# Residual additions of six tiles moved from VectorE to GpSimd at the end of a feed-forward

## The chip, the cores and the metric

One NeuronCore of one Trainium2 chip runs the whole program. The metric is the device time of one execution in microseconds (us); for a set of executions the median is given. Of the core's engines five matter here: TensorE (PE, matrix products and transposes), VectorE (DVE), ScalarE (ACT), GpSimd (POOL) and SyncE (SP), whose queue issues the transfers between memory and SBUF. Each engine works through its own program in order, and the engines are tied together by semaphores only. The profile names GpSimd POOL and VectorE DVE.

## What is computed

The program is one transformer block on a sequence of 1024 tokens with 1024 features, all in float32. It is a feed-forward, a mixer (sparse attention beside a recurrence), a cross attention to a memory, and a second feed-forward. Each is wrapped in norms and a residual. The change is in the end of the first feed-forward and in the norm that the mixer begins with:

```python
h = rms_norm(x, ffn1_pre_g[l])
x = x + 0.5 * rms_norm(swiglu(h, ffn1_w_gate[l], ffn1_w_up[l], ffn1_w_down[l]), ffn1_post_g[l])
h = rms_norm(x, mix_pre_g[l])
proj = h @ w_in[l]

def rms_norm(x, g):
    xf = x.astype(jnp.float32)
    y = xf * lax.rsqrt(jnp.mean(xf * xf, -1, keepdims=True) + NORM_EPS)
    return (y * g.astype(jnp.float32)).astype(x.dtype)
```

## The kernel before

`ffn_products` is called twice: for the first feed-forward (tag `f1`, with `next_gain`, so `after` is true) and for the second (tag `f2`, without it). The down projection lies token by feature: 8 tiles of 128 tokens by 1024 features, and each tile is two parts of 512 features (`m` = 2t and 2t + 1), which TensorE leaves in PSUM. Every float32 product is made of three passes over operands split into a high and a low half (`hi`, `lo`).

The end of the function is a software pipeline over tiles, written out by hand. In `step` s the engines do the following, each in this order:

- VectorE adds the last partial products of tile s onto `y` (L609, two instructions), then for tile s - 1 takes the reciprocal of the root (L619), multiplies by it and by the gain (L695, "scale") and adds the residual x in place (L699, "residual"); then for tile s - 2 the reciprocal of the next norm's root (L619) and its product with the gain (L705, "norm"); then for tile s - 3 the low halves of the transposed tile (L636, two instructions).
- ScalarE squares and sums tile s (L425) and takes the root (L427); then does the same over x of tile s - 1, for which it waits on the semaphore `x_added`; then copies the high halves of the transposed tile s - 3 to `hi` (L437, two instructions).
- TensorE transposes a tile when its norm is written (L781, eight matmuls) and then makes the products of the tile four further on (L715 to L717).
- SyncE stores each x tile when `x_added` has counted it, and loads x of tile t + 3 into the place of tile t - 1.

x lies in the four places of `f_raw`, scaled `y` in `one_y`, and the gains and normed tiles in `f_work`. Behind the stage there is a barrier of all engines (`core.clear`), and then `project_and_prepare` (names `fr_...`) begins. GpSimd has no work in this stage. Its float32 additions of another stage (L1248, 128 x 256, names `ar_...`) are the only two-input work that it does.

Of the kernel before, what the change touches and what calls it, by code (L numbers as in the profile page):

```python
# [16 lines left out]
ALU = mybir.AluOpType  # L17
# [85 lines left out]
def ffn_products(core, tag, w_gate, w_up, w_down, kept_dram, hi, lo, y, consts, x_in, x_out, post_gain, first_gain=None, next_gain=None, work=None,  # L103
# [8 lines left out]
    nc = core.nc  # L112
    ident, eps = consts["ident"], consts["eps"]
    F = w_gate.shape[1]
    PAIRS = F // (2 * P)
    LAST = PAIRS - 1
    before, after = first_gain is not None, next_gain is not None
    A11, A12, S2, S3, A22, S1, S4 = range(7)
    C11, C21, C22, C12 = range(4)
# [2 lines left out]
    with core.stage() as ctx:  # L122
# [60 lines left out]
        x_loaded = core.sems(f"{tag}_x_loaded", 4)  # L183
# [7 lines left out]
        scaled, x_added = core.sem(f"{tag}_scaled"), core.sem(f"{tag}_x_added")  # L191
        block = core.block(ctx)
# [7 lines left out]
        def split_at(i, s):  # L200
            return i * 7 + (s - 2)
# [13 lines left out]
        def of_tile(t):  # L215
            return slice(t * P, (t + 1) * P)
# [16 lines left out]
        def x_of(t):  # L233

            return raw[:].rearrange("p n (a k) f -> p (n a) (k f)", a=2)[:, t % 4, :]

        def turn_bank(n, t, h):
            bank = (4, 5, 6, 7) if n == 0 else (0, 1, 6, 7)
            return ps[:, bank[t % 2 * 2 + h], :].rearrange("p (k t) -> p k t", t=P)
# [5 lines left out]
        def _(sp):  # L245
# [13 lines left out]
            def keep(i, e):  # L259
                j, h = (0, 1, 1, 0)[e], (0, 0, 1, 1)[e]  # L260
                sp.wait_ge(prod_done, silu_at(i, e))
                sp.dma_start(kept_dram[bass.ds(i * 2 * P + j * P, P), h * HALF:(h + 1) * HALF], c[:, e, 1, :]).then_inc(kept[e], 16)

            def load_d(p):
                sp.dma_start(raw_d, d_dram[:, bass.ds(p * 2, 2), :]).then_inc(d_in, 16)

            def load_a(p):
                sp.dma_start(raw_a, a_dram[:, bass.ds(p * 2, 2), :]).then_inc(a_in, 16)
# [21 lines left out]
            for e in (C11, C21, C22):  # L290
                keep(1, e)
            with sp.Fori(2, LAST) as i:
                keep(i - 1, C12)
                sp.wait_ge(split_lo, split_at(i, A22))
                load_pair(i + 1)
                for e in (C11, C21, C22):
                    keep(i, e)
            keep(LAST - 1, C12)
            sp.wait_ge(split_lo, split_at(LAST, A22))
            load_d(0)  # L300
# [3 lines left out]
            for e in (C11, C21, C22, C12):  # L304
                keep(LAST, e)
            with sp.Fori(0, LAST - 1) as p:
                sp.wait_ge(down_lo, p * 4 + 2)
                load_d(p + 1)
                sp.wait_ge(down_lo, p * 4 + 4)
                load_a(p + 1)  # L310
            sp.wait_ge(down_lo, 4 * LAST - 2)
            load_d(LAST)
# [184 lines left out]
        def _(dve):  # L497
# [103 lines left out]
            def add(p, m, first=False):  # L601
                dve.wait_ge(dn_mm[m % 4], p * 4 + (m // 4 + 1))
                if first:
                    if m >= 8:
                        e = m // 2 - 4
                        dve.wait_ge(kept[e], kept_before(PAIRS, e))
                    nc.vector.tensor_copy(y[part(m)], down_bank(m)).then_inc(added[m % 4], 1)  # L607
                else:
                    nc.vector.tensor_tensor(y[part(m)], down_bank(m), y[part(m)], ALU.add).then_inc(added[m % 4], 1)  # L609
# [7 lines left out]
            def inverse(n, t):  # L617
                dve.wait_ge(rooted[n], t + 1)
                nc.vector.reciprocal(stats[:, n, 2, t:t + 1], stats[:, n, 1, t:t + 1]).then_inc(inverted[n], 1)  # L619
                dve.wait_ge(inverted[n], t + 1)  # L620
                return stats[:, n, 2, t:t + 1]
# [10 lines left out]
            def turned_lo(n, t):  # L632
                for h in range(2):
                    dve.wait_ge(hi_done[n], 2 * t + h + 1)
                    at = (slice(None), slice(4 * h, 4 * h + 4), of_tile(t))
                    nc.vector.tensor_tensor(lo[at], turn_bank(n, t, h), hi[at].bitcast(F32), ALU.subtract).then_inc(lo_done[n], 1)  # L636
# [48 lines left out]
            for step in range(TT + 3):  # L685
                t = step
                if t < TT:
                    add(LAST - 1, 2 * t)
                    add(LAST - 1, 2 * t + 1)
                t = step - 1  # L690
                if 0 <= t < TT:
                    rstd = inverse(1, t)
                    if t == 0:
                        dve.wait_ge(gains_in, 32 if after else 16)
                    nc.vector.scalar_tensor_tensor(out=y[:, t, :], in0=y[:, t, :], scalar=rstd, in1=g_post,  # L695
                                                   op0=ALU.mult, op1=ALU.mult).then_inc(scaled, 1)
                    dve.wait_ge(x_loaded[t % 4], 16 * (t // 4 + 1))
                    dve.wait_ge(scaled, t + 1)
                    nc.vector.tensor_tensor(x_of(t), x_of(t), y[:, t, :], ALU.add).then_inc(x_added, 1)  # L699
                t = step - 2  # L700
                if after and 0 <= t < TT:
                    rstd = inverse(2, t)
                    if t >= 2:
                        dve.wait_ge(turned[2], t - 1)
                    nc.vector.scalar_tensor_tensor(out=xn[:, t % 2, :], in0=x_of(t), scalar=rstd, in1=g_next,  # L705
                                                   op0=ALU.mult, op1=ALU.mult).then_inc(normed[2], 1)
                t = step - 3
                if after and t >= 0:
                    turned_lo(2, t)

        @block.tensor
        def _(pe):
# [2282 lines left out]
def block_kernel(nc, a, out):  # L2995
# [22 lines left out]
    with ExitStack() as ctx:  # L3018
        consts = make_consts(core, ctx, f["ident_"])

        def ffn(n, hi, lo, y, x_in, x_out, **gains):
            ffn_products(core, f"f{n}", f[f"ffn{n}_w_gate"], f[f"ffn{n}_w_up"], f[f"ffn{n}_w_down"], act, hi, lo, y, consts,
                         x_in, x_out, f[f"ffn{n}_post_g"], **gains)
# [92 lines left out]
```

## Time and profile before

| | |
|---|---|
| time, median of 3 executions | 2843.67 us (2841.96 to 2845.47) |
| the profiled execution: its own time | 2842.68 us |
| the profiled execution: span of the trace | 2840.8 us |
| mean granted TensorE clock | 0.976 |
| PE busy | 2683.6 us (94%) |
| DVE busy | 1756.1 us (62%) |
| ACT busy | 968.1 us (34%) |
| POOL busy | 88.0 us (3%) |

The shares are means over stages with different limits. TensorE is the busy engine of the whole, and a single stage can be held by another one. The stage with the change lies between 672 and 735 us of the span. In the timeline a row gives the start, the duration, the engine, the line and the operation, and in brackets the idle time before it with what ended it. Starts of successive instructions on an engine are closer than their durations, since they overlap a little.

### The profile page before, as it was taken

What the parts mean: (1) busy time and instruction counts of PE and PEld (TensorE: products, weight loads), DVE (VectorE), ACT (ScalarE), POOL (GpSimd) and SP (SyncE); (2) the same over time, 40 slices, a digit from 0 to 9 for tenths busy, and PEclk for the clock granted to TensorE, in tenths of its full rate; (3) what the DMA queues carried; (4) which work ended last, traced back from release to release, by engine and by line L of the source; (5) the groups of instructions that cost most, each with busy time, mean ns of one, the idle gap of its engine ahead of it and who ended that gap; (6) DMA issues with size and microseconds to landing.
All of it is one profiled execution on the core that took longest, in us unless ns stands there. A gap on an engine that the chain in (4) does not pass through costs nothing. (4 is left out here: it accounts for less than half of the span.)

```text
span 2840.8 us, 47378 instructions
## 1 busy us (share of the span) xinstructions
PE 2683.6 (94%) x19368; PEld 2214.9 (78%) x19368; DVE 1756.1 (62%) x2869; ACT 968.1 (34%) x1731; POOL 88.0 (3%) x121
## 2 busy tenths in 40 slices
PE   6999999999799999699999998899997999999998
PEld 5888887887577778588888886687775888887887
DVE  5866665767444472277777775753444856666666
ACT  4332222113333433244444444442432323222122
POOL 0000000000000000111111110000000000000000
PEclk9999999999899999799999999999998999999999
DMA  4222223224423385611111110530031222223224
GB/s 138 82 85 74 74 85 107 104 103 153 102 86 97 107 271 140 164 43 40 40 35 29 36 40 26 212 127 1 30 119 56 82 89 85 74 73 119 103 89 156
DMA packets 230632, 260.91 MB, mean 92 GB/s; under 512 B 63426, under 2 KB 186560, under 8 KB 230464
## 3 DMA queue, kind: packets, MB, share of 16 engines
q1 hardware_dynamic: 228880, 256.91, 28.3%
q8 instruction: 124, 2.03, 0.3%
q10 hardware_dynamic: 1584, 1.60, 0.2%
q14 instruction: 44, 0.36, 0.0%
HBM read 189.17 MB, written 64.06 MB: 89 GB/s over the span
## 5 line engine op out<-in xcount | busy, mean ns | idle before, releaser
L715 PE MATMUL f_ps<-hi,f_wh 128*128 128x512 f32 x768 | 302.1, 393 | 19.3 <-DVE f_wl L501 11.9
L717 PE MATMUL f_ps<-hi,f_wl 128*128 128x512 f32 x768 | 300.8, 392 | 0.0
L715 PE MATMUL f_ps<-f_t1h,f_wh 128*128 128x512 f32 x480 | 187.1, 390 | 0.0
L716 PE MATMUL f_ps<-f_t1l,f_wh 128*128 128x512 f32 x480 | 186.8, 389 | 0.0
L715 PEld LDWEIGHTS f_ps<-hi,f_wh 128*128 128x128 f32 x768 | 145.5, 189 | 52.4 <-issue 10.7
L2051 PE MATMUL fr_dense_ps<-hi,fr_wh 128*128 128x512 f32 x400 | 167.0, 417 | 7.1 <-DVE fr_wl L2342 7.1
L717 PEld LDWEIGHTS f_ps<-hi,f_wl 128*128 128x128 f32 x768 | 145.5, 189 | 30.4
L715 PE MATMUL f_ps<-f_t2h,f_t3h 128*128 128x512 f32 x384 | 151.6, 395 | 7.8 <-DVE one_y L607 3.7
L2052 PE MATMUL fr_dense_ps<-one_lo,fr_wh 128*128 128x512 f32 x400 | 156.8, 392 | 0.0
L2053 PE MATMUL fr_dense_ps<-hi,fr_wl 128*128 128x512 f32 x400 | 156.8, 392 | 0.0
L716 PE MATMUL f_ps<-f_t2l,f_t3h 128*128 128x512 f32 x384 | 150.9, 393 | 0.0
L717 PE MATMUL f_ps<-f_t2h,f_t3l 128*128 128x512 f32 x384 | 150.7, 393 | 0.0
L716 PE MATMUL f_ps<-two_lo,f_wh 128*128 128x512 f32 x384 | 150.5, 392 | 0.0
L716 PE MATMUL f_ps<-one_lo,f_wh 128*128 128x512 f32 x384 | 150.4, 392 | 0.0
L609 DVE TENSOR_TENSOR y<-f_ps,y 128x512 f32<-128x512 f32 x144 | 99.2, 690 | 61.7 <-PE f_ps L717 61.7
L549 DVE TENSOR_TENSOR one_y<-f_ps,one_y 128x1024 f32<-128x1024 f32 x60 | 72.5, 1222 | 100.4 <-PE f_ps L717 100.4
L549 DVE TENSOR_TENSOR y<-f_ps,y 128x1024 f32<-128x1024 f32 x60 | 72.5, 1222 | 100.3 <-PE f_ps L717 100.3
L609 DVE TENSOR_TENSOR one_y<-f_ps,one_y 128x512 f32<-128x512 f32 x144 | 98.7, 689 | 56.0 <-PE f_ps L717 56.0
L717 PE MATMUL f_ps<-f_t1h,f_wh 128*128 128x512 f32 x320 | 124.5, 389 | 0.0
L2740 PE MATMUL mt_d_ps<-mt_wh,hi 128*128 128x512 f32 x224 | 94.6, 423 | 20.4 <-DVE two_lo L2933 19.0
L2342 DVE TENSOR_TENSOR fr_wl<-one_y,fr_wh 128x1024 fp32r<-128x1024 f32 x41 | 50.1, 1221 | 96.3 <-ACT fr_wh L2207 96.2
L715 PEld LDWEIGHTS f_ps<-f_t1h,f_wh 128*128 128x128 f32 x480 | 90.1, 188 | 18.5
(419 smaller groups left out, 6458.8 us busy)
## 6 DMA issues: line engine op xcount, KB each, us to landing
one_y<-in_w_in SPq DMA_DIRECT2D x25, 512.0 KB, 4.4
f_raw<-in_ffn_w_gate SPq DMA_DIRECT2D x11, 1024.0 KB, 5.4
f_raw<-in_ffn_w_up SPq DMA_DIRECT2D x11, 1024.0 KB, 7.9
act<-one_y SPq DMA_DIRECT2D x44, 256.0 KB, 2.1
f_raw<-in_ffn_w_down SPq DMA_DIRECT2D x11, 1024.0 KB, 4.9
f_raw<-act SPq DMA_DIRECT2D x11, 1024.0 KB, 4.8
early<-in_ffn_w_gate SPq DMA_DIRECT2D x11, 1024.0 KB, 5.4
early<-in_ffn_w_up SPq DMA_DIRECT2D x11, 1024.0 KB, 7.9
```

Of the source, the lines that this page charges most:

```text
L549: nc.vector.tensor_tensor(out, a, b, op).then_inc(joined, 1)
L609: nc.vector.tensor_tensor(y[part(m)], down_bank(m), y[part(m)], ALU.add).then_inc(added[m % 4], 1)
L715: nc.tensor.matmul(out, wh, xh, start=start, stop=False)
L716: nc.tensor.matmul(out, wh, xl, start=False, stop=False)
L717: return nc.tensor.matmul(out, wl, xh, start=False, stop=stop)
L2051: nc.tensor.matmul(dense_ps[:, b, cols], w_hi[:, b, k, :], hi[:, k, cols], start=(k == 0), stop=False)
L2052: nc.tensor.matmul(dense_ps[:, b, cols], w_hi[:, b, k, :], lo[:, k, cols], start=False, stop=False)
L2053: mm = nc.tensor.matmul(dense_ps[:, b, cols], w_lo[:, b, k, :], hi[:, k, cols], start=False, stop=(k == KD - 1))
L2342: nc.vector.tensor_tensor(w_lo[:, c % 2], raw[:, c % 2], w_hi[:, c % 2].bitcast(F32), ALU.subtract).then_inc(lo_split, 1)
L2740: mm = nc.tensor.matmul(bank(n, b), lhsT[:, k, at], rhs[:, k, to], start=(k == 0 and x_ == 0), stop=(k == KD - 1 and x_ == 2))
```

## The change

For the first feed-forward `BY_POOL` is 6, for the second 0. GpSimd gets a program of its own for the stage: for each of the tiles 0 to 5 it waits until x is loaded and `y` is scaled, and adds. VectorE keeps the additions of tiles 6 and 7, and ahead of tile 6 it waits until all six of GpSimd have been counted on `x_added`, which both engines increment.

```diff
+    BY_POOL = 6 if next_gain is not None else 0
...
                     nc.vector.scalar_tensor_tensor(out=y[:, t, :], in0=y[:, t, :], scalar=rstd, in1=g_post,
                                                    op0=ALU.mult, op1=ALU.mult).then_inc(scaled, 1)
-                    dve.wait_ge(x_loaded[t % 4], 16 * (t // 4 + 1))
-                    dve.wait_ge(scaled, t + 1)
-                    nc.vector.tensor_tensor(x_of(t), x_of(t), y[:, t, :], ALU.add).then_inc(x_added, 1)
+                    if t >= BY_POOL:
+                        dve.wait_ge(x_loaded[t % 4], 16 * (t // 4 + 1))
+                        dve.wait_ge(scaled, t + 1)
+                        if t == BY_POOL and BY_POOL:
+                            dve.wait_ge(x_added, BY_POOL)
+                        nc.vector.tensor_tensor(x_of(t), x_of(t), y[:, t, :], ALU.add).then_inc(x_added, 1)
...
+        @block.gpsimd
+        def _(pool):
+            for t in range(BY_POOL):
+                pool.wait_ge(x_loaded[t % 4], 16 * (t // 4 + 1))
+                pool.wait_ge(scaled, t + 1)
+                nc.gpsimd.tensor_tensor(x_of(t), x_of(t), y[:, t, :], ALU.add).then_inc(x_added, 1)
```

VectorE's program in step 4 of the stage, before (lines of the kernel before):

```order
L609 TENSOR_TENSOR one_y<-f_ps,one_y 128x512 [waits f1_dn_mm0]
L609 TENSOR_TENSOR one_y<-f_ps,one_y 128x512 [waits f1_dn_mm1]
L619 RECIPROCAL f_stats<-f_stats 128x1 [waits f1_rooted1]
L695 SCALAR_TENSOR_TENSOR one_y<-one_y,f_stats,f_work 128x1024 [waits f1_inverted1]
L699 TENSOR_TENSOR f_raw<-f_raw,one_y 128x1024 [waits f1_scaled,f1_x_loaded3]
L619 RECIPROCAL f_stats<-f_stats 128x1 [waits f1_rooted2]
L705 SCALAR_TENSOR_TENSOR f_work<-f_raw,f_stats,f_work 128x1024 [waits f1_turned2,f1_inverted2]
L636 TENSOR_TENSOR one_lo<-f_ps,hi 128x4x128 [waits f1_hi_done2] x2
```

The same step on VectorE now (lines of the changed kernel, one to four further on):

```order
L610 TENSOR_TENSOR one_y<-f_ps,one_y 128x512 [waits f1_dn_mm0]
L610 TENSOR_TENSOR one_y<-f_ps,one_y 128x512 [waits f1_dn_mm1]
L620 RECIPROCAL f_stats<-f_stats 128x1 [waits f1_rooted1]
L696 SCALAR_TENSOR_TENSOR one_y<-one_y,f_stats,f_work 128x1024 [waits f1_inverted1]
L620 RECIPROCAL f_stats<-f_stats 128x1 [waits f1_rooted2]
L709 SCALAR_TENSOR_TENSOR f_work<-f_raw,f_stats,f_work 128x1024 [waits f1_turned2,f1_inverted2]
L637 TENSOR_TENSOR one_lo<-f_ps,hi 128x4x128 [waits f1_hi_done2] x2
```

The residual has gone from between scale and norm, so the reciprocal and the norm of the tile before follow scale directly.

GpSimd's program from the stage's beginning to the next stage's now, of which only the last two rows were there before:

```order
L720 ISA
L720 TENSOR_TENSOR f_raw<-f_raw,one_y 128x1024 [waits f1_scaled,f1_x_loaded0]
L720 TENSOR_TENSOR f_raw<-f_raw,one_y 128x1024 [waits f1_scaled,f1_x_loaded1]
L720 TENSOR_TENSOR f_raw<-f_raw,one_y 128x1024 [waits f1_scaled,f1_x_loaded2]
L720 TENSOR_TENSOR f_raw<-f_raw,one_y 128x1024 [waits f1_scaled,f1_x_loaded3]
L720 TENSOR_TENSOR f_raw<-f_raw,one_y 128x1024 [waits f1_scaled,f1_x_loaded0]
L720 TENSOR_TENSOR f_raw<-f_raw,one_y 128x1024 [waits f1_scaled,f1_x_loaded1]
L123 UNCONDITIONAL_BRANCH
L2046 UNCONDITIONAL_BRANCH [waits barrier_Pool_Activation_PE_DVE_SP_gather]
L2048 MEMSET fr_w_full 64x512
```

The six additions now stand alone on GpSimd, each behind the scale of its own tile. ScalarE's program in a step has the same rows as before (here step 4's, lines of the changed kernel):

```order
L426 ACTIVATE f_junk,f_stats<-one_y 128x1024 [waits f1_summed1,f1_added1,f1_added0]
L428 ACTIVATE f_stats<-f_stats,eps 128x1 [waits f1_summed1]
L426 ACTIVATE f_junk,f_stats<-f_raw 128x1024 [waits f1_summed2,f1_x_added]
L428 ACTIVATE f_stats<-f_stats,eps 128x1 [waits f1_summed2]
L438 CAST hi<-f_ps 128x4x128 [waits f1_turned2]
L438 CAST hi<-f_ps 128x4x128
```

Nothing moved on it: the square over x, which waits on `x_added`, still stands ahead of the copies to `hi`.

## Rows read from the trace of the kernel before

**Rows 1.** Timeline, VectorE, step 4 of the stage (start us, us)

```profile
694.98 1.28 DVE L609 TENSOR_TENSOR one_y<-f_ps,one_y 128x512 f32<-128x512 f32 x2
696.17 0.15 DVE L619 RECIPROCAL f_stats<-f_stats 128x1 f32<-128x1 f32 x1
696.36 1.28 DVE L695 SCALAR_TENSOR_TENSOR one_y<-one_y,f_stats,f_work 128x1024 f32<-128x1024 f32 x1
697.75 1.23 DVE L699 TENSOR_TENSOR f_raw<-f_raw,one_y 128x1024 f32<-128x1024 f32 x1
698.89 0.16 DVE L619 RECIPROCAL f_stats<-f_stats 128x1 f32<-128x1 f32 x1
699.09 1.28 DVE L705 SCALAR_TENSOR_TENSOR f_work<-f_raw,f_stats,f_work 128x1024 f32<-128x1024 f32 x1
701.00 1.29 DVE L636 TENSOR_TENSOR one_lo<-f_ps,hi 128x512 fp32r<-128x512 f32 x2 [0.63 <-ACT hi L437]
702.20 1.28 DVE L609 TENSOR_TENSOR one_y<-f_ps,one_y 128x512 f32<-128x512 f32 x2
```

**Rows 2.** Timeline, ScalarE, the same step

```profile
699.01 1.06 ACT L425 ACTIVATE f_junk<-f_raw 128x1024 bf16<-128x1024 f32 x1 [1.19 <-DVE f_raw L699]
...
700.19 0.29 ACT L427 ACTIVATE f_stats<-f_stats,eps 128x1 f32<-128x1 f32 x1
700.40 1.05 ACT L437 CAST hi<-f_ps 128x512 fp32r<-128x512 f32 x2
```

**Rows 3.** Busy time by windows: PE, PEld, DVE, ACT, POOL, clock, DMA

```profile
694.98:702.20 7.22, 7.22 (x39) 6.09 (x38) 6.42 (x10) 3.85 (x8) 0.00 (x0) 1.00 0.52 178
...
716.64:723.85 7.21, 1.77 (x8) 1.57 (x8) 6.41 (x10) 3.85 (x8) 0.00 (x0) 0.76 0.18 73
```

**Rows 4.** Timeline, VectorE, scales of tiles 0 and 1, norm of tile 0

```profile
679.90 1.28 DVE L695 SCALAR_TENSOR_TENSOR one_y<-one_y,f_stats,f_work 128x1024 f32<-128x1024 f32 x1 [3.99 <-DMA f_work<-in_mix_pre_g]
...
683.82 1.29 DVE L695 SCALAR_TENSOR_TENSOR one_y<-one_y,f_stats,f_work 128x1024 f32<-128x1024 f32 x1
...
686.55 1.28 DVE L705 SCALAR_TENSOR_TENSOR f_work<-f_raw,f_stats,f_work 128x1024 f32<-128x1024 f32 x1
```

**Rows 5.** Timeline, TensorE, transposes of tiles 0 and 1

```profile
687.89 1.09 PE L781 MATMUL f_ps<-ident,f_work 128*128 128x128 f32 x8 [2.15 <-DVE f_work L705]
...
694.30 1.03 PE L781 MATMUL f_ps<-ident,f_work 128*128 128x128 f32 x8
```

**Rows 6.** One line: GpSimd's additions elsewhere, duration ns min/median/max

```profile
L1248 POOL TENSOR_TENSOR ar_LTm<-ar_GB,ar_m_lev x80: 715/732/1129, 1194.6 to 1700.0; 128x256 f32<-128x256 f32 x80
```

**Rows 7.** Groups of GpSimd instructions by shape: busy us, mean ns

```profile
L1242 POOL MEMSET ar_win<- 128x512 f32 x1 | 0.5, 526 | 0.0
...
L1241 POOL MEMSET ar_M<- 128x256 f32 x1 | 0.3, 312 | 441.7 <-POOLq L69 441.7
...
L1243 POOL MEMSET ar_kc<- 128x2 f32 x1 | 0.1, 97 | 0.0
```

**Rows 8.** Timeline, VectorE and GpSimd, near 1314 us

```profile
1314.06 0.42 DVE L1574 TENSOR_TENSOR ar_L<-ar_ps,ar_m_low 128x256 f32<-128x256 f32 x1 [0.38 <-PE ar_ps L1347]
...
1315.61 0.84 DVE L1621 TENSOR_TENSOR ar_TT<-ar_TT,ar_eye 128x256 f32<-128x256 f32 x1
...
1314.56 0.73 POOL L1248 TENSOR_TENSOR ar_T<-ar_L,ar_m_one 128x256 f32<-128x256 f32 x1 [53.79 <-DVE ar_L L1574]
1315.25 0.92 POOL L1248 TENSOR_TENSOR ar_LTm<-ar_GB,ar_m_lev 128x256 f32<-128x256 f32 x1
```

**Rows 9.** Timeline, VectorE and GpSimd, near 1463 us

```profile
1463.30 0.41 DVE L1619 TENSOR_TENSOR ar_TT<-ar_GB,ar_m_one 128x256 f32<-128x256 f32 x1
...
1463.46 0.84 POOL L1248 TENSOR_TENSOR ar_T<-ar_L,ar_m_one 128x256 f32<-128x256 f32 x1 [0.49 <-DVE ar_L L1574]
```

**Rows 10.** Timeline, VectorE's last of the stage, ScalarE's first of the next

```profile
734.64 0.68 DVE L636 TENSOR_TENSOR one_lo<-f_ps,hi 128x512 fp32r<-128x512 f32 x1
...
738.15 1.99 ACT L2207 CAST fr_wh<-one_y 128x1024 fp32r<-128x1024 f32 x2 [3.66 <-PEq L69]
```

**Rows 11.** Busy time by windows, the next stage's first 14 us

```profile
738.00:752.00 14.00, 11.50 (x43) 9.37 (x44) 3.29 (x5) 1.99 (x2) 0.52 (x1) 0.78 0.68 129
```

## The prediction

> **What bounds the stage now.** I read the windows of the stage first, then the timeline of one step on VectorE, then the same step on ScalarE, and last every place in the trace where GpSimd adds. TensorE leads the whole kernel, but in this stage the beat is VectorE's: one step takes 7.22 us, VectorE is busy 6.42 us of it, and the step repeats unchanged when TensorE has run dry (1.77 us busy) [rows 3]. TensorE's own work on a tile takes 694.30 - 687.89 = 6.41 us [rows 5].
>
> VectorE still idles 0.63 us in the step, and it waits there for ScalarE [rows 1]. So the closed loop is not VectorE's work alone. From the step's start to the end of scale is 697.64 - 694.98 = 2.66 us. The residual starts 0.11 later and takes 1.23 [rows 1]. ScalarE's square over x starts 0.03 behind it (699.01 against 698.98), the copy to hi comes 1.39 after that (700.40), VectorE's low half 0.60 later (701.00), and the next step 1.20 later (702.20) [rows 1, 2]. The sum is 2.66 + 0.11 + 1.23 + 0.03 + 1.39 + 0.60 + 1.20 = 7.22. The residual is a link of that loop, because on ScalarE the copies for tile s - 3 stand behind the square over x of tile s - 1, and VectorE's low half waits for the copies. The norm (1.28 us) lies beside this loop, not on it.
>
> **What the change does to the loop.** It takes 1.23 us of work from VectorE but leaves the residual where it was in the chain: scale, then residual, then ScalarE. The link 0.11 + 1.23 becomes a hand-over to GpSimd plus GpSimd's duration P. The hand-over: a DVE addition ends at 1314.48 and GpSimd starts at 1314.56, 0.08 us [rows 8]. A step of the loop is then 5.96 + P, and it changes by P - 1.26.
>
> P is not in the trace at 128 x 1024. GpSimd's 128 x 256 addition has a median of 732 ns [rows 6], and 0.73 us where nothing disturbs it [rows 8]. From above, four of these are 2.92 us. From below, its MEMSET grows by 526 - 312 = 214 ns for 256 elements [rows 7]; an addition that grew no faster would take 0.73 + 3 x 0.214 = 1.37. MEMSET reads nothing, so I hold to the upper end and take off only the fixed part, which MEMSET of 2 elements shows as 0.097 [rows 7]: P = 2.92 - 3 x 0.10 = 2.62 us. A larger fixed part makes P smaller.
>
> The Trainium skill (GPSIMD Engine Reference, "Performance versus the Vector engine") gives 4497 ns for an addition of 2048 float32, and calls GpSimd about half as fast as VectorE at it. Half of that is an estimate of 2.25 us for this tile, and by it the sum below would be +4.3 us. The trace agrees with the direction, 0.73 against VectorE's 0.42 at 256 elements [rows 8].
>
> **Does the freed VectorE run undisturbed?** Near 1315 us VectorE's addition of two SBUF operands took 0.84 [rows 8], while the same shape took 0.41 elsewhere [rows 9]. It ended (1316.45) 0.28 behind GpSimd's (1316.17), and GpSimd's took 0.92 instead of 0.73. So of two such additions one waits almost until the other is done, and a held VectorE instruction ends 0.13 less than its own length behind GpSimd's end. Scale and norm also have two SBUF operands; the additions of L609 and the low halves of L636 have one, the other lies in PSUM. The Trainium skill (SBUF, "Who interferes with whom") says it as a rule: a VectorE instruction with two SBUF inputs and a GpSimd instruction that reads SBUF exclude each other, and whoever starts first holds the port to its end. The trace agrees, by the 0.84 and 0.92. A rule without this exclusion would take the first term below from +1.05 to below nothing.
>
> **Steps 1 and 2, where time could be won.** Scale of tile 0 ends at 681.18 [rows 4], GpSimd's addition runs 681.26 to 683.88. VectorE, freed of its residual, does the two additions of step 2 and asks for scale of tile 1 near 682.5, 1.3 us before its old start, but is held: it ends at 683.88 + 1.28 - 0.13 = 685.03, against 685.11 before [rows 4]. GpSimd takes tile 1 from 685.11 to 687.73. Norm of tile 0 needs ScalarE's root, which comes at 683.88 + 0.03 + 1.39 = 685.30, so it asks after GpSimd has begun and is held again: it ends at 687.73 + 1.15 = 688.88, against 687.83 [rows 4]. That is +1.05 us, and TensorE, which idles 2.15 us for this norm [rows 5], idles 3.2.
>
> **Steps 3 to 6.** Each has GpSimd's addition in the loop: 4 x (2.62 - 1.26) = 5.44 us. ScalarE's other square of the step (1.39) ends before GpSimd does and is hidden by it. TensorE's 6.41 per tile stays under the new step of 8.58. The norm, held by GpSimd, ends near 3.8 us behind scale; the low half starts 4.7 behind it, so it is covered.
>
> **Steps 7 to 10** are as before: residuals 6 and 7 are VectorE's, and the added wait for six counts on x_added was met a step earlier. The stores follow x_added in order. The load of x for tile 4 waits for norm 0 and starts some 1.1 us later, and its tile is wanted more than 10 us after that. GpSimd's empty slot has nothing else in it. The six instructions left out of VectorE need no other cover. The barrier and the next stage start 2.8 us after VectorE's last low half [rows 10] and move with it.
>
> **Sum.** 1.05 + 5.44 = +6.5 us. P stands in it six times (twice in the first term, four times in the second), so in general it is 6.5 + 6 x (P - 2.62): -1.0 at P = 1.37, +8.3 at 2.92. The profiled execution took 2842.68 us, 1.9 more than its span. 2842.68 + 6.5 = 2849.2. The median of the executions shown lies 0.99 above it, so the forecast for a median is 2850.2. What this kernel's timing can tell from no change I take as 0.2%, 5.7 us; the sum passes it where P is over 2.49.
>
> **The rivals.**
>
> 1. *VectorE's norm gets the port first in steps 3 to 6.* Behind scale GpSimd starts at +0.08. The norm follows at +0.11, as behind the residual now (699.09 against 698.98 [rows 1]), with the reciprocal overlapped. 0.03 us decide. Near 1463 us VectorE was 0.16 ahead and ran its full 0.41, GpSimd took 0.84 instead of 0.73: the port was free 0.27 after VectorE's start, 0.14 short of its length [rows 9]. By this a norm ahead holds GpSimd for 0.03 + 1.14 = 1.17 us a step, four times 4.7: +11.2, 2854.9 us. For it speaks how narrow the lead is, against it that GpSimd has the lead. In step 2 it cannot happen, the norm is late there by ScalarE.
> 2. *The other side: GpSimd's addition is mostly a fixed cost.* Were P the 0.73 of 256 elements, the loop would lose 0.53 a step, and the sum would be 6.5 + 6 x (0.73 - 2.62) = -4.8, 2838.9 us. The sign turns at P = 1.54. MEMSET's growth from 97 to 526 ns speaks against it [rows 7]. Beating the kernel before by 0.2% would need P under 0.6.
> 3. *TensorE loses its clock, or GpSimd starts slowly.* TensorE would idle 2.2 us in each step of 8.6. At 1.77 us busy of 7.21 the granted clock fell to 0.76 on the mean, at full work it was 1.00 [rows 3]. At 1.2 GHz a tile's 6.41 would be 12.8, more than the step by 4.2, in four steps some 17 us. Alternatively the first addition pays once. GpSimd's first addition of this stage stands behind an instruction that readies it (ISA in its program) by some 670 us. The Trainium skill (GPSIMD Engine Reference, "Instruction dispatch") has about 6 us for the first call into freshly loaded code; no row here shows it.
>
> **How the numbers follow.** The forecast's case (GpSimd first, P from 2.0 to 2.9) has a chance of 0.54 and gives 2846.5 to 2852; the part of it over 0.2% has 0.30, the part under has 0.24, since P sits near the edge. Rival 1 has 0.28, all of it slower. Rival 2 with all P under 2.0 has 0.10: 0.02 faster, 0.08 within 0.2%. Rival 3 has 0.08, slower. Slower is 0.30 + 0.28 + 0.08 = 0.66, same 0.32, faster 0.02. The range goes from P = 2.0 (+2.8, 2846.5) to rival 1 with P = 2.8 (+12.3, 2856); it leaves out rival 2 and rival 3. Where the next stage's first matmuls meet the clock's return (0.78 on the mean of its first 14 us [rows 11]) can move either figure by about a microsecond.
>
> **What would show it.** In the changed trace: six GpSimd additions of 2.3 to 2.9 us; steps 3 to 6 of 8.3 to 8.9 us from one pair of L610 to the next, with ScalarE's square over x waiting for GpSimd; VectorE's wait before L637 grown from 0.63 to above 2 us or taken up by a norm of some 3.6 us; scale of tile 1 shown as some 2.5 us long; step 7 at 7.2 us again. Wrong I would be if the additions are under 1.6 us, if GpSimd's rows are near 3.8 us and the norms 1.28 (rival 1), if a matmul in steps 3 to 6 takes double, or if the next stage takes back what this one loses.

## The result and the profile after

The changed kernel takes 2847.78 us, the kernel before 2841.97 us (medians of 20 executions each, taken in turn). The ratio is 1.0020 with a 95% interval of 1.0014 to 1.0026, so the change costs 5.8 us. Forecast were 6.5 us more and 2850.2 in the range 2846.5 to 2856.0; the before it was added to, 2843.67, lies 1.7 above the median of the larger set.

The profiled executions have spans of 2846.1 and 2840.8 us. A whole kernel of this length varies by some microseconds from one execution to the next, so from here on the stage is measured inside one trace: from the start of the first scale (L695 before, L696 now) to the start of the last low halves (L636, L637). That is 734.03 - 679.90 = 54.13 us before and 738.04 - 678.59 = 59.45 now, 5.32 us more. In these two traces the rest of the span evens out: the first scale comes 1.31 earlier, and what lies behind the stage takes 1.3 longer.

The page of the changed kernel shows where work went. VectorE should have lost 6 x 1.23 = 7.4 us and has 4.5 more than before (1756.1), GpSimd has 14.1 more (88.0):

```profile
PE 2684.6 (94%) x19368; PEld 2215.1 (78%) x19368; DVE 1760.6 (62%) x2863; ACT 967.5 (34%) x1731; POOL 102.1 (4%) x127
```

VectorE in step 4 of the changed kernel, in the timeline, beside [rows 1]:

```profile
695.41 1.28 DVE L610 TENSOR_TENSOR one_y<-f_ps,one_y 128x512 f32<-128x512 f32 x2
696.61 0.15 DVE L620 RECIPROCAL f_stats<-f_stats 128x1 f32<-128x1 f32 x1
696.80 1.29 DVE L696 SCALAR_TENSOR_TENSOR one_y<-one_y,f_stats,f_work 128x1024 f32<-128x1024 f32 x1
698.00 0.16 DVE L620 RECIPROCAL f_stats<-f_stats 128x1 f32<-128x1 f32 x1
698.19 3.51 DVE L709 SCALAR_TENSOR_TENSOR f_work<-f_raw,f_stats,f_work 128x1024 f32<-128x1024 f32 x1
702.64 1.29 DVE L637 TENSOR_TENSOR one_lo<-f_ps,hi 128x512 fp32r<-128x512 f32 x2 [0.94 <-ACT hi L438]
703.84 1.28 DVE L610 TENSOR_TENSOR one_y<-f_ps,one_y 128x512 f32<-128x512 f32 x2
```

The step is 703.84 - 695.41 = 8.43 us long instead of 7.22. The residual is gone, and the norm that follows directly has grown from 1.28 to 3.51: what VectorE was to be spared, it now spends on a norm that has started and is held until GpSimd's addition is done. GpSimd's rows of tiles 1 to 3:

```profile
683.66 2.34 POOL L720 TENSOR_TENSOR f_raw<-f_raw,one_y 128x1024 f32<-128x1024 f32 x1 [1.23 <-DVE one_y L696]
689.82 2.38 POOL L720 TENSOR_TENSOR f_raw<-f_raw,one_y 128x1024 f32<-128x1024 f32 x1 [3.81 <-DVE one_y L696]
698.23 2.39 POOL L720 TENSOR_TENSOR f_raw<-f_raw,one_y 128x1024 f32<-128x1024 f32 x1 [6.04 <-DVE one_y L696]
```

Scale ends at 698.09, GpSimd starts 0.14 later and ends at 700.62; the norm ends at 701.70, 1.08 behind it. ScalarE in the same step, beside [rows 2]:

```profile
700.65 1.06 ACT L426 ACTIVATE f_junk<-f_raw 128x1024 bf16<-128x1024 f32 x1 [2.40 <-POOL f_raw L720]
...
702.04 1.05 ACT L438 CAST hi<-f_ps 128x512 fp32r<-128x512 f32 x2
```

It waits for GpSimd now, 0.03 behind its end, and its copies are what VectorE's low halves wait for. The chain is the one of before with a slower link. The windows of steps 4 and 5 and of step 7, beside [rows 3]:

```profile
695.41:703.84 8.43, 8.31 (x45) 6.81 (x43) 7.42 (x9) 3.85 (x8) 2.39 (x1) 1.00 0.41 142
703.84:712.25 8.41, 6.58 (x33) 5.25 (x32) 7.40 (x10) 3.85 (x8) 2.37 (x1) 1.00 0.35 123
720.66:727.86 7.20, 1.77 (x8) 1.57 (x8) 6.42 (x10) 3.85 (x8) 0.00 (x0) 0.60 0.19 74
```

Step 7, where the residual is VectorE's again, is 7.20 long (7.21 before). VectorE's busy time per step has risen from 6.42 to 7.42 with less to do; 2.2 us of what is shown as busy is the norm being held. The first steps, beside [rows 4]:

```profile
681.18 2.33 DVE L696 SCALAR_TENSOR_TENSOR one_y<-one_y,f_stats,f_work 128x1024 f32<-128x1024 f32 x1
...
684.17 2.91 DVE L709 SCALAR_TENSOR_TENSOR f_work<-f_raw,f_stats,f_work 128x1024 f32<-128x1024 f32 x1
```

Scale of tile 1 and norm of tile 0 are both held, 2.33 and 2.91 instead of 1.28. Behind them TensorE's transpose starts (its row, beside [rows 5], and the window after it):

```profile
687.14 1.20 PE L792 MATMUL f_ps<-ident,f_work 128*128 128x128 f32 x8 [3.19 <-DVE f_work L709]
```

```profile
687.10:690.40 3.30, 3.26 (x14) 2.78 (x15) 3.23 (x6) 1.82 (x5) 0.58 (x1) 0.64 1.03 292
```

TensorE idled 3.19 us instead of 2.15, as forecast, and then something came that was not in the sum: the granted clock in the 3.3 us behind is 0.64, that is 1.2 GHz for most of it, where before it was 1.00 all through. This is inside step 3, and the starts of the 128 x 512 matmuls stand 0.43 us apart there, 0.23 later in the same step.

### The profile page after: what moved, and what is told of

It is laid out like the page before. It is cut to its first block and busy times, and to the rows that moved or that the text cites. A ratio compares the mean times of both kernels' runs of the same rounds, so it can differ in the third digit from the quotient of the medians.

```text
span 2846.1 us, 47378 instructions
## 1 busy us (share of the span) xinstructions
PE 2684.6 (94%) x19368; PEld 2215.1 (78%) x19368; DVE 1760.6 (62%) x2863; ACT 967.5 (34%) x1731; POOL 102.1 (4%) x127
## 5 line engine op out<-in xcount | busy, mean ns | idle before, releaser
L610 DVE TENSOR_TENSOR y<-f_ps,y 128x512 f32<-128x512 f32 x144 | 99.1, 689 | 61.6 <-PE f_ps L728 61.6
L610 DVE TENSOR_TENSOR one_y<-f_ps,one_y 128x512 f32<-128x512 f32 x144 | 98.7, 689 | 56.0 <-PE f_ps L728 56.0
L727 PEld LDWEIGHTS f_ps<-f_t1l,f_wh 128*128 128x128 f32 x480 | 90.4, 188 | 18.7
```

Of the source, the lines that this page charges most:

```text
L727: nc.tensor.matmul(out, wh, xl, start=False, stop=False)
```

## The experiments

Each run e1 to e10 was executed 11 times (e2 5 times) in turn with the kernel before, in three sets (e1 to e4, e5 to e8, e9 and e10); the changed kernel's row is that of the section before. "Stage" is the length defined above, from one trace of each kernel.

| run | stage us | against 54.13 | ratio to before, 95% interval |
|---|---|---|---|
| changed kernel | 59.45 | +5.32 | 1.0020 (1.0014 to 1.0026) |
| e1_two_tiles | 55.23 | +1.10 | 1.0002 (0.9993 to 1.0011) |
| e2_late_start | 64.13 | +10.00 | 1.0035 (1.0022 to 1.0049) |
| e3_half_add | 52.99 | -1.14 | 0.9995 (0.9986 to 1.0004) |
| e4_thin_add | 47.76 | -6.37 | 0.9979 (0.9970 to 0.9988) |
| e5_copies_first_before | 49.83 | -4.30 | 0.9984 (0.9975 to 0.9993) |
| e6_copies_first_after | 54.02 | -0.11 | 0.9995 (0.9986 to 1.0004) |
| e7_lows_first_after | 55.13 | +1.00 | 1.0005 (0.9996 to 1.0014) |
| e8_late_six | 52.67 | -1.46 | 0.9997 (0.9988 to 1.0006) |
| e9_lows_first_to_seven | 49.56 | -4.57 | 0.9986 (0.9977 to 0.9995) |
| e10_middle_five | 48.65 | -5.48 | 0.9980 (0.9971 to 0.9989) |

One per mille is 2.84 us. In every row the stage's difference lies inside the interval of the whole kernel, so within some 2.6 us (3.8 for e2) what the stage loses or wins goes through to the end. The five runs whose interval holds 1 are told apart by the stage alone.

### Is the residual a link of the loop, and what is it worth per microsecond?

e1 leaves GpSimd only the tiles ahead of the loop:

```diff
-    BY_POOL = 6 if next_gain is not None else 0
+    BY_POOL = 2 if next_gain is not None else 0
```

> BY_POOL is 2 instead of 6, so GpSimd adds for tiles 0 and 1 alone. The stage from the first scale to the start of the last low halves took 54.13 us before and 59.45 with six tiles. Theory A (the residual is a link of the loop from step 3 on, each step there pays 1.2 us, steps 1 and 2 together 0.57): 54.7, and 0.0% to 0.05% over the kernel before. Theory B (each tile on GpSimd costs the same, 5.32 / 6 = 0.89): 55.9.

Measured was 55.23, between the two. Up to the additions of step 3 the stage is the changed kernel's (8.43 and 8.42 behind the first scale; before 7.85), so steps 1 and 2 cost 0.57 as in theory A, and steps 5 to 7 are 7.22 long again. The other 0.5 came in step 4:

```profile
694.45 0.68 DVE L610 TENSOR_TENSOR one_y<-f_ps,one_y 128x512 f32<-128x512 f32 x1
695.57 0.69 DVE L610 TENSOR_TENSOR one_y<-f_ps,one_y 128x512 f32<-128x512 f32 x1 [0.44 <-PE f_ps L728]
```

VectorE waits for a product here, since TensorE's matmuls behind its idle time of 2.76 us ran at the lower clock (granted 0.65 in the 3.3 us from 687.4). The two rows of its timeline are a matmul behind the transpose and one 3.3 us later:

```profile
688.66 0.63 PE L727 MATMUL f_ps<-f_t1l,f_wh 128*128 128x512 f32 x1
...
691.94 0.39 PE L726 MATMUL f_ps<-f_t2h,f_t3h 128*128 128x512 f32 x1
```

So theory B, the same cost for every tile, falls: two tiles ahead of the loop cost 0.57, each of the four in the loop 1.20, and a longer TensorE wait can add half a microsecond through the clock. In the changed kernel no L610 of the stage waits for a product; that last part is covered by the longer steps.

e3 and e4 leave the hand-overs as they are and shorten GpSimd's addition; they leave out the rest of the residual. This is e3's edit, and e4 has `0:2` in place of `0:HALF`:

```diff
-                nc.gpsimd.tensor_tensor(x_of(t), x_of(t), y[:, t, :], ALU.add).then_inc(x_added, 1)
+                nc.gpsimd.tensor_tensor(x_of(t)[:, 0:HALF], x_of(t)[:, 0:HALF], y[:, t, 0:HALF], ALU.add).then_inc(x_added, 1)
```

> The changed kernel with GpSimd adding only features 0 to 511 of each of its six tiles (the other half of the residual is left out). Theory A (GpSimd's duration stands in the stage six times, and breaks even near 1.2 us): the addition takes 1.28 us, a step of 3 to 6 takes 7.3, steps 1 and 2 gain 1.6, the stage 52.9, 1.2 under the kernel before. Theory B (a fixed cost of the hand-over between engines is what is lost): steps near 8.4 still, the stage over 58.

> The changed kernel with GpSimd adding only 2 features of each of its six tiles (the rest of the residual is left out), so that the loop keeps its hand-overs but almost no duration. Theory A: the loop would take 6.2 us, less than TensorE's 6.41 for a tile, so TensorE becomes the bound: steps 3 to 6 at 6.4, the stage 48.5 to 49.5, 0.15% to 0.2% under the kernel before. Theory B (hand-overs are what is lost): the stage no shorter than 54.

The half addition took 1.29 us, the step 7.33, the stage 52.99 (52.9 expected). The thin one, of 2 features, took 0.20, the step 6.23 to 6.33, the stage 47.76, less than the 48.5 to 49.5 expected: steps 1 and 2 gained 2.64 (5.21 us from the first scale to the additions of step 3), and steps 3 and 4 took the loop's own 6.23, not yet TensorE's 6.33 to 6.42 from one transpose to the next. Theory B of both, that the hand-over itself is what is lost, falls. In step 5 of the thin run VectorE and GpSimd read:

```profile
701.29 1.30 DVE L709 SCALAR_TENSOR_TENSOR f_work<-f_raw,f_stats,f_work 128x1024 f32<-128x1024 f32 x1
...
701.32 0.20 POOL L720 TENSOR_TENSOR f_raw<-f_raw,one_y 128x2 f32<-128x2 f32 x1 [6.08 <-DVE one_y L696]
```

With 0.20, 1.29 and 2.38 us for 2, 512 and 1024 elements, GpSimd's addition is 0.19 us plus 2.13 ns an element. From 1024 to 512 elements the stage fell by 6.46 us for 1.09 us of duration, 5.9 times as much: the factor 6 of the prediction.

### Who gets the port?

In the changed kernel the norm starts 0.04 us ahead of GpSimd (698.19 against 698.23), and still it is the norm that waits. The port is the access to SBUF that, as the prediction has it, the two engines share. e2 lets GpSimd ask a little later (`late` is a small tile of its own):

```diff
                 pool.wait_ge(scaled, t + 1)
+                nc.gpsimd.memset(late[:, 64 * t:64 * t + 64], 0.0)
                 nc.gpsimd.tensor_tensor(x_of(t), x_of(t), y[:, t, :], ALU.add).then_inc(x_added, 1)
```

> The changed kernel with one GpSimd MEMSET of 128 x 64 between the wait for scale and each addition, so that GpSimd asks for its operands some 0.15 us later than now, when VectorE's norm starts 0.04 us ahead of it and yet waits for it. Theory A (the port goes to whoever asks first, and VectorE lost by a few hundredths): the norms of steps 3 to 6 fall back to 1.28 us, GpSimd's additions there rise from 2.38 to about 3.4, a step takes 9.6 instead of 8.41, the stage 64.5. Theory B (GpSimd always wins, whoever starts first): norms stay near 3.5 us, only the MEMSET's own 0.15 is added per step, the stage 60.4. The first addition comes right behind the instruction that readies GpSimd for it: if that costs once, tile 0's is longer by some microseconds, otherwise 2.4.

The timeline of VectorE and GpSimd in step 4 of that run:

```profile
699.32 1.28 DVE L710 SCALAR_TENSOR_TENSOR f_work<-f_raw,f_stats,f_work 128x1024 f32<-128x1024 f32 x1
704.87 1.29 DVE L638 TENSOR_TENSOR one_lo<-f_ps,hi 128x512 fp32r<-128x512 f32 x2 [4.27 <-ACT hi L439]
```

```profile
699.33 0.15 POOL L721 MEMSET f_late<- 128x64 f32 x1 [6.01 <-DVE one_y L697]
699.43 3.42 POOL L722 TENSOR_TENSOR f_raw<-f_raw,one_y 128x1024 f32<-128x1024 f32 x1
```

The norm is back at 1.28, GpSimd's addition takes 3.42, and VectorE's wait before the low halves is 4.27. The step is 9.5 us, the stage 64.13 (64.5 expected). This is rival 1 of the prediction, brought about by a tenth of a microsecond: with 0.11 of a lead VectorE wins, with 0.04 GpSimd does. Theory B falls. The instruction that readies GpSimd stands at 679.8 to 679.9 us in this run and the first addition right behind it, at 679.94; it took 2.40, as long as the undisturbed additions of the changed kernel (2.34 to 2.41), so no such start cost shows here. In the changed kernel that instruction stands at 3.1 us, and the first addition took 2.41.

### Is it the order on ScalarE that puts the residual in the loop?

e5 swaps two pieces of ScalarE's program in the kernel before, and e6 in the changed kernel; both compute the whole:

```diff
+                t = step - 3
+                if after and t >= 0:
+                    turned_hi(2, t)
                 t = step - 1
                 if after and 0 <= t < TT:
                     act.wait_ge(x_added, t + 1)
                     rms(2, t, x_of(t), 1.0 / D, 0)
-                t = step - 3
-                if after and t >= 0:
-                    turned_hi(2, t)
```

> The kernel before with one change on ScalarE: in each step the copies to hi of tile s - 3 stand ahead of the square over x of tile s - 1. Theory A (the residual is in the loop only because of that order): the wait of 0.63 us ahead of the low halves goes, a step is VectorE's own work, 1.20 + 0.19 + 1.39 + 1.15 + 0.19 + 1.20 + 1.20 = 6.52 instead of 7.22, the stage 50.0 instead of 54.13, 0.15% under the kernel before. Theory B (ScalarE's copies come late for another reason): steps stay at 7.2, the stage at 54.

The end of step 4 on VectorE in e5:

```profile
699.18 1.28 DVE L705 SCALAR_TENSOR_TENSOR f_work<-f_raw,f_stats,f_work 128x1024 f32<-128x1024 f32 x1
700.39 1.28 DVE L636 TENSOR_TENSOR one_lo<-f_ps,hi 128x512 fp32r<-128x512 f32 x2
701.59 1.28 DVE L609 TENSOR_TENSOR one_y<-f_ps,one_y 128x512 f32<-128x512 f32 x2
```

The wait of 0.63 is gone, the step is 6.51 and the stage 49.83 (50.0 expected): three lines in another place bring 4.3 us, on the kernel before and without GpSimd.

> The changed kernel with the same swap on ScalarE. GpSimd's addition is then no link of the loop of the low halves. Theory A (the norm, held by GpSimd until it is done, takes its place on VectorE): 2.66 + 0.14 + 2.37 + 1.08 - 0.08 + 1.20 = 7.4 a step in steps 3 to 6, 6.5 in steps 7 and 8, the stage 54 to 54.5. Theory B (exclusion by GpSimd costs nothing once the order is right): TensorE's 6.41 a step, the stage 50.

```profile
698.86 3.51 DVE L709 SCALAR_TENSOR_TENSOR f_work<-f_raw,f_stats,f_work 128x1024 f32<-128x1024 f32 x1
702.29 1.27 DVE L637 TENSOR_TENSOR one_lo<-f_ps,hi 128x512 fp32r<-128x512 f32 x2
```

With six tiles on GpSimd the same swap leads to a step of 7.41 and a stage of 54.02. The low halves no longer wait for ScalarE; they stand directly behind a norm of 3.51 us. That is 4.2 us more than e5. 3.6 of it lie in steps 3 to 6 (7.41 against 6.51), and there the low halves wait for no copy: the exclusion, that one engine is held while the other adds, keeps the freed VectorE from being faster. The other 0.6 are those of steps 1 and 2.

### Can the freed time be used at all?

e7 gives VectorE work with one operand in SBUF to do beside GpSimd's addition, in place of the norm: on top of e6, `turned_lo(2, step - 3)` stands ahead of the norm of `step - 2`.

> As the run before, and on VectorE the low halves of tile s - 3 (one operand in SBUF, one in PSUM) stand ahead of the norm of tile s - 2, beside GpSimd's addition. Theory A: what was waiting for GpSimd in vain is filled with work that doesn't exclude it, 2.66 + 0.14 + 2.37 + 1.08 - 0.08 = 6.2 a step on VectorE, so that TensorE's 6.41 is the bound in steps 3 to 6; with the 0.6 of steps 1 and 2 the stage takes 50 to 50.5. Theory B (low halves are held by GpSimd too): steps of 7.4 or more, the stage over 54.

e8 has the order of e7, with `for t in range(2, TT)` on GpSimd and tiles 0 and 1 on VectorE.

> As the run before, but with tiles 2 to 7 on GpSimd and tiles 0 and 1 on VectorE, so that the norm for which TensorE idles isn't held and TensorE doesn't idle longer than in the kernel before. Theory A: the 0.57 of steps 1 and 2 and the matmuls at half clock behind the longer idle time go, steps 3 on at TensorE's 6.4, the stage 49 to 49.8, the shortest that computes the whole. Theory B (GpSimd on the last two tiles lies on the closing chain, where nothing is left to put beside it, 1.2 us a tile): the stage 51 to 52.

The short steps came in both: 6.2 to 6.4 us, near TensorE's own 6.33 to 6.42 for a tile, with norms of 1.57 us at most and low halves of 1.29 beside GpSimd's addition. Only step 4 of e7 took 7.72, with a wait of 1.42 for a product. The stages missed the expectation by 4.6 and 2.9 us. The end of e7 shows one reason:

```profile
725.15 1.28 DVE L712 SCALAR_TENSOR_TENSOR f_work<-f_raw,f_stats,f_work 128x1024 f32<-128x1024 f32 x1
729.11 1.29 DVE L637 TENSOR_TENSOR one_lo<-f_ps,hi 128x512 fp32r<-128x512 f32 x2 [2.68 <-ACT hi L438]
730.32 0.15 DVE L620 RECIPROCAL f_stats<-f_stats 128x1 f32<-128x1 f32 x1
730.50 1.28 DVE L712 SCALAR_TENSOR_TENSOR f_work<-f_raw,f_stats,f_work 128x1024 f32<-128x1024 f32 x1
```

Where no additions are left, each norm now stands behind the low halves of the tile before it, so transposes and copies of the last tiles run one after the other, 5.36 us a tile. I had carried over the steady step and not looked at the end. It is so in e8 too, and there it is the whole miss: from the scale of tile 7 to the last low halves e7 and e8 both take 13.28 us, though tile 7 is added by VectorE in the one and by GpSimd in the other, against 9.26 in e10 below. Theory B of e8 came near in its number (51 to 52), but GpSimd's last tiles, its reason, are not what costs. e9 and e10 put the norm first again from step 8 on; e10 gives GpSimd `range(2, 7)` and VectorE tiles 0, 1 and 7:

```diff
+                if after and step >= TT and 0 <= step - 2 < TT:
+                    norm(step - 2)
+                if after and step - 3 >= 0:
+                    turned_lo(2, step - 3)
+                if after and step < TT and 0 <= step - 2 < TT:
+                    norm(step - 2)
```

> As e7_lows_first_after, but from step 8 on VectorE does the norm ahead of the low halves again. Theory A (e7 reached its short steps, 6.35 us, but lost them at the end, where no tile is left to do beside and the last two norms stood behind the low halves of two tiles before them, 5.36 us a tile instead of 2.7): the stage 51 to 51.5 instead of 55.13. Theory B (what e7 lost was lost in steps 3 and 4, by TensorE at half clock behind its longer idle time, which cost a wait of 1.42 us for a product there): the stage at 54 or more.

> As the run before, with tiles 2 to 6 alone on GpSimd and tiles 0, 1 and 7 on VectorE. Theory A: no hold of the norm that TensorE idles for, TensorE's 6.35 a step in steps 3 to 7, and the last residual on the faster engine: the stage 48.5 to 49.2, against 49.83 with the swap on ScalarE alone, 0.18% under the kernel before. Theory B (GpSimd's part brings nothing over the swap on ScalarE): 49.8 or more.

e9 took 49.56, at least 1.4 less than theory A had it. It also differs from e7 in the clock, though the two programs are the same up to step 7: behind an idle time of 2.52 us the matmuls kept their pace in e9, behind 2.88 in e7 they didn't (6.41 us from one transpose to the next, 7.98 in e7), and e7's scale of tile 3 came 1.47 later for it. So of the 5.57 between e7 and e9 some 4 are the end and 1.5 the clock. By that 1.5 two traces of one program lay apart in the stage, so a smaller difference between kernels whose clocks differ says little; in e5 and e10 the clock behind that idle time stays at 1.00. e10 took 48.65 (48.5 to 49.2 expected). Its step on VectorE:

```profile
703.36 1.56 DVE L708 SCALAR_TENSOR_TENSOR f_work<-f_raw,f_stats,f_work 128x1024 f32<-128x1024 f32 x1
704.85 1.38 DVE L610 TENSOR_TENSOR one_y<-f_ps,one_y 128x512 f32<-128x512 f32 x2
...
708.30 1.29 DVE L637 TENSOR_TENSOR one_lo<-f_ps,hi 128x512 fp32r<-128x512 f32 x2 [0.68 <-ACT hi L438]
```

It has the shortest stage and the lowest ratio of those that compute the whole: 2837.94 us against 2843.18 in its set, 0.9980. But 4.3 of its 5.5 us of stage are e5's, three lines on ScalarE. GpSimd and the new order on VectorE together add 1.2 us to that in the stage, which the timing of the whole kernel can't tell (0.9980 and 0.9984, each known to 0.0009). The new order on VectorE without GpSimd was not run, so how the 1.2 divides between the two isn't shown.

## Why the prediction was right, by its steps

**The loop.** The step was put together as 2.66 + hand-over + P + 0.03 + 1.39 + 0.60 + 1.20. Measured, it is 2.68 + 0.14 + 2.39 + 0.03 + 1.39 + 0.60 + 1.20 = 8.43. e5, e6 and the pair e3 and e4 each confirm it from another side: order, exclusion, duration.

**The size of P.** Taken was 2.62, measured 2.38. The fixed part is 0.19 us, where the MEMSET of two elements had suggested 0.10; the rest of the extrapolation holds (0.19 + 256 x 2.13 ns = 0.74, against 0.73 [rows 8]). In the sum this is 6 x 0.24 = 1.4 us too much. The estimate from the Trainium skill, half of 4497 ns = 2.25 us (GPSIMD Engine Reference, "Performance versus the Vector engine"), would have been 0.13 too little; the measurement lies between the two.

**The hand-over.** Taken was 0.08, measured 0.14, which four steps make 0.24. With both corrected the forecast's formula gives 6.5 - 1.4 + 0.2 = 5.3, and the stage shows 5.32.

**Steps 1 and 2.** +1.05 at P = 2.62 is +0.57 at 2.38, and 0.57 was measured (8.42 against 7.85 from the first scale to the additions of step 3). Nothing was won there, for the reason given: scale of tile 1 was asked for early and held. That it fits to 0.01 is in part luck: the two hand-overs there took 0.16 and 0.15 instead of 0.08, 0.15 more together, and the two held instructions ended 1.07 and 1.08 behind GpSimd instead of 1.15, 0.15 less.

**Exclusion.** Norms of about 3.6 us and a scale of 2.5 were forecast, 3.5 and 2.33 came. VectorE's wait before the low halves did not grow beyond 2 us (0.94), because the held norm takes it up, the other form that was named. That one excludes the other for a whole instruction is as the Trainium skill has it (SBUF — State Buffer, "Who interferes with whom"), and the trace agrees, by the norm of 3.51 and e2's addition of 3.42 us. By the Trainium skill the port goes to whoever issues first. By the starts that the trace gives, the first gets it in e2 and not in the changed kernel (0.04 us); the trace has no row for who issued first.

**Rival 1** was 0.07 us away, as e2 shows. The forecast had GpSimd ahead by 0.03; by start times it was behind by 0.04 and got the port all the same. The case came out right, but the argument for it did not hold: that part is luck. The size of the rival was nearly right, +11.2 for a stage that e2 has at +10.0.

**Rival 2** falls: the fixed part is 0.19 us and the rest grows with the elements. Its direction was sound, as e3 and e4 show: the formula 6.5 + 6 x (P - 2.62) gives -1.5 at 1.29 us, where -1.14 was measured, and -8.0 at 0.20, where it was -6.37; so short an addition gains 2.64 in steps 1 and 2 and not the 3.8 of the formula. **Rival 3** came in small: the clock fell for about 3.3 us, once, behind TensorE's longer idle time for the norm of tile 0, and cost nothing in the changed kernel. It fell in step 3, so one sign of being wrong that was named, a matmul in steps 3 to 6 that takes double, did show there, without the loss that it stood for. In steps 4 to 6 TensorE idled 1.83 us at a time at most (2.2 were forecast), and the windows of steps 4 and 5 show 1.00.

**Two ends.** The stage's +5.3 lies inside the interval of the whole kernel's +5.8 (4.0 to 7.4 us). That the stage's loss goes through to the end holds. On which side of the prediction's line of 0.2% (5.7 us) the change lies is not told: 5.8 is at the line, and the interval reaches to both sides. With P at 2.38 the sum itself would have stood just under it.

## What to carry to other kernels

Before work is moved from a busy engine to an idle one, look at whether it lies beside the others or in a chain with them: here the addition stayed between scale and square whichever engine did it, so only its duration counted, and 1.23 became 2.38. The busy engine is not freed by the length of what it gives away as long as its next instruction also has two operands in SBUF; put one with an operand in PSUM beside GpSimd's addition. And look first for a queue that waits for a new value ahead of work whose input has long been there: moving the copies ahead of the square was worth 4.3 us, more than GpSimd ever brought. An order that is right in the steady step is to be followed through the last steps too.

## What was not expected of the hardware

- VectorE started 0.04 us (0.03 in e6) ahead of GpSimd and still waited for all of its addition; with a lead of 0.11 it did not wait. So within some hundredths of a microsecond the starts in a trace do not tell who gets the port. Whether the operands are asked for later than the start or GpSimd is preferred when the two are that close is open; finer steps of the lead were not tried.
- A VectorE instruction held by GpSimd shows as busy, not as waiting: 3.5 us for a norm of 1.28. The profile's busy share of VectorE rose while its work fell.
- TensorE's idle time for the norm of tile 0 was 2.76 us in e1, 2.77 in e2, 2.88 in e7 and 3.19 in the changed kernel, and behind each of them the matmuls ran at 1.2 GHz for some 3 us. Behind 2.15 (before), 2.38 (e6) and 2.52 (e9) they kept 2.4 GHz. With the same program up to there this idle time was 2.76 in e1 and 3.19 in the changed kernel, and it was 2.88 in e7 and 2.52 in e9, of which only e7 lost the clock: it varies with when the gains, which the first scale waits for, arrive beside TensorE's work, so the same program can fall on either side.
